# A two-layer hybrid decoder trunk: stick and differential attention in joint steps, stick q and k from stationary weights, the rotation on VectorE

## The chip, the cores and the metric

The kernel runs on one core of one Trainium2 chip. The time is the device time of one execution in microseconds, median of three runs.

## What is computed

x is 256 tokens by 1024, the depth is two layers. All products are float32 in the reference.

```python
f = swiglu(rms_norm(h, ffn1_pre_g[i]), ffn1_w_gu[i], ffn1_w_down[i])
h = h + 0.5 * rms_norm(f, ffn1_post_g[i])
u = rms_norm(h, mix_pre_g[i])
sb_q, sb_k, sb_v, df_q, df_k, df_v, g_sb, g_df = jnp.split(u @ w_in[i], split_at, axis=-1)
o_sb = stick_breaking_attention(sb_q, sb_k, sb_v)      # 8 heads of 64
dq, dk = rope(df_q, positions), rope(df_k, positions)  # 4 heads, 2 x 64
o_df = rms_norm(differential_attention(dq, dk, df_v, lam), ...) * (1.0 - lam_init)
merged = sigmoid(g_sb) * (o_sb @ w_branch_sb[i]) + sigmoid(g_df) * (o_df @ w_branch_diff[i])
h = h + rms_norm(merged @ w_out[i], mix_post_g[i])
```

The second FFN and a gated embedding follow in each layer. Stick attention masks strictly (key before query), differential attention causally (key not after query), with a softmax.

## The kernel before

The engines' programs are written out by hand, with semaphores; the order in the code is the order of each queue. There are 8 PSUM banks of 512 columns. Weights come in units of 2048 columns by 128 rows through three slots. SyncE loads a unit (`raw`), ScalarE writes its rounded high part (`high`, L646, four pieces of 512, scaled by the norm's gain), VectorE the rest (`low`, L1084), and TensorE starts the unit when `split_done` says so (`begin`). A slot is free for ScalarE when TensorE has counted the unit in `units_used`. A product is exact by three passes: high x high, high x low, low x high (`exact`, L1473 to L1475). In the FFN the weights are the stationary side instead (L1591, L1601): a pass of 512 columns takes high weights against both halves of the inputs, a pass of 256 low weights against the high half; the two halves land side by side in a bank and are added later.

The mixer runs units m = 0 to 19 of w_in, two to each block of 512 output columns (j = m // 2), then m = 20 to 27 of the branch and output weights. The blocks are in the order stick q, k, v, diff q, k, v, gates. For q and k, `wide` has the inputs stationary, so the result has tokens as rows. ScalarE copies it to `tmp` (`keep`), scaled by the norm factor of the row. For diff, GpSimd rotates it (`rope`, L577 to L585, in `tmp` and `glu`). TensorE transposes it (`turn_four`, L1692) and ScalarE or VectorE copies the result to `sbq_t`, `sbk_t`, `dfq_t`, `dfk_t`. v is kept by VectorE (L1314).

Small steps stand between the big ones. `middle(i, m)` comes after the first token tile of unit m, `behind(i, m)` after its second. Stick pairs of heads take scores (L1709, L1712), then on ScalarE abs, exp and ln (L792 to L796), on VectorE the cap and the split (L1241 to L1255), then `stick_later` (L1723), the weights (L788), then the values (L1736) and their split `os_hi`, `os_lo`. Two stick steps share banks 0 and 1. A diff head takes a mask matmul (L1698), scores (L1749, L1752), the row maximum on VectorE (L1323), exp on ScalarE (L804), the mix (L1344), the transposes (L1759), their copy `mixed_t` (L813), the values (L1767 to L1770), their squares, GpSimd's scale and VectorE's normed output (L1278).

```python
SB_SCORE = {12 + 6 * n: n for n in range(PAIRS)}
SB_LATER = {15 + 6 * n: n for n in range(PAIRS)}
SB_VALUE = {17 + 6 * n: n for n in range(PAIRS)}
DF_Z0, DF_T0, DF_P0 = 12, 13, 14
```

A stick slot is 2m for `middle` and 2m + 1 for `behind`. The diff heads start every second unit from 12, and the stick pairs every third unit from 6. The mixer's semaphore for ready norm factors is `pre_scale`; GpSimd derives `r_query` from them (`query_scale`, L598).

Of the kernel before, what the change touches and what calls it, by code (L numbers as in the profile page):

```python
# [76 lines left out]
def trunk_kernel(nc, a, out):  # L77
    with ExitStack() as ctx:
# [82 lines left out]
        ident_b = sb("ident_b", [P, P], BF16)  # L161
# [3 lines left out]
        mask_df = sb("mask_df", [P, SEQ], BF16)  # L165
# [15 lines left out]
        slab_c = tmp[:, :, W:D]  # L181

# [42 lines left out]
        kept_dve = sem("kept_dve")  # L225
# [3 lines left out]
        sb_turned = sem("sb_turned")  # L229
# [12 lines left out]
        d_score = sem("d_score")  # L242
        d_max = sem("d_max")
# [71 lines left out]
        OUT_COLS = slice(384, W)  # L315
        both_scores = ps[:, 0:2, 0:384]
        both_outs = ps[:, 0:2, OUT_COLS]
# [68 lines left out]
        def _(sp_):  # L386
# [56 lines left out]
            for i in range(DEPTH):  # L443
# [27 lines left out]
        def _(pool):  # L471
# [33 lines left out]
            for c in (0, P):  # L505

                last = pool.affine_select(out=mask_df[:, c:c + P], in_=mask_df[:, c:c + P],
                                          compare_op=ALU.is_ge, fill=NEG, base=0, pattern=[[-1, P]],
                                          channel_multiplier=1)
            last.then_inc(const_all, 1)  # L510
# [58 lines left out]
            def rope(i, k):  # L569

                for t in range(TT):
                    pool.wait_ge(kept_act, 16 * i + 2 * (2 + k) + t + 1)
                    if k or t:
                        pool.wait_ge(roped, 4 * i + 2 * k + t)
                    x = slab[:, t, :].rearrange("p (g c) -> p g c", c=64)
                    y = rope_b[:, t, :].rearrange("p (g c) -> p g c", c=64)
                    pool.tensor_tensor(slab_c[:, t, :].rearrange("p (g c) -> p g c", c=64), x,  # L577
                                       rope_c[:, t:t + 1, :].to_broadcast([P, 8, 64]), ALU.mult)
                    pool.tensor_tensor(y[:, :, 0:32], x[:, :, 32:64],
                                       rope_s[:, t:t + 1, 0:32].to_broadcast([P, 8, 32]), ALU.mult)  # L580
                    pool.tensor_tensor(y[:, :, 32:64], x[:, :, 0:32],
                                       rope_s[:, t:t + 1, 32:64].to_broadcast([P, 8, 32]), ALU.mult
                                       ).then_inc(rope_parts, 1)
                    pool.wait_ge(rope_parts, 4 * i + 2 * k + t + 1)
                    pool.tensor_tensor(slab[:, t, :], slab_c[:, t, :], rope_b[:, t, :], ALU.add).then_inc(roped, 1)  # L585

            for i in range(DEPTH):
# [11 lines left out]
                pool.wait_ge(rope_ready, 2)  # L599
# [18 lines left out]
        def _(act):  # L618
# [196 lines left out]
            def diff_mid(i, m):  # L815

                if m >= DF_P0 and (m - DF_P0) % 2 == 0 and (m - DF_P0) // 2 < DF_HEADS:
                    hd = (m - DF_P0) // 2
                    act.wait_ge(d_value, DF_HEADS * i + hd + 1)
                    if hd:  # L820
                        act.wait_ge(d_square, DF_HEADS * i + hd)
# [1137 lines left out]
```

## Time and profile before

| what | value |
|---|---|
| median of 3 runs | 1186.8 us (1186.26 to 1187.11) |
| the profiled execution | 1187.24 us |
| its span | 1185.2 us |
| PE busy | 1173.8 us (99%) |
| VectorE (DVE) busy | 848.7 us (72%) |
| ScalarE (ACT) busy | 719.9 us (61%) |
| GpSimd (POOL) busy | 92.9 us (8%) |
| mean granted TensorE clock | 0.999 |

The span goes from the first to the last instruction. Duration of a matmul in a row is from its issue to its modelled end, so neighbours overlap; the distance between starts is what counts. An fp32 matmul of the scores or values stands twice in the trace (four rows for two); a transpose stands once. The first layer's mixer goes from about 205 to 367 us, the second's from about 789 to 952.

### The profile page before, as it was taken

Reading aid. Unit: us, or ns where it says so; the run is one execution under the profiler, and the core shown is the slowest. Engines: PE = TensorE matmul, PEld = TensorE weight load, DVE = VectorE, ACT = ScalarE, POOL = GpSimd, SP = SyncE. Lnnn points to the kernel's source line nnn. Section 1 sums busy time; section 2 is a strip of 40 time slices with the busy share of each in tenths; the row PEclk is TensorE's granted clock in tenths of the full one; section 3 lists DMA queues with packets and bytes.
Section 4 is the critical chain, followed back from the end, with each engine's and each line's share of the span. In section 5 each row is a group of like instructions: output and inputs, shape, how many; then the busy total and the mean of one; then the engine's idle time right before and its main releaser. Section 6 shows DMA issues by size and latency. Waiting matters only on the chain.

```text
span 1185.2 us, 17137 instructions
## 1 busy us (share of the span) xinstructions
PE 1173.8 (99%) x6013; PEld 984.4 (83%) x6013; DVE 848.7 (72%) x1235; ACT 719.9 (61%) x1163; POOL 92.9 (8%) x157
## 2 busy tenths in 40 slices
PE   8999999999999999999999999999999999999997
PEld 7888888888788888888888888888877888888886
DVE  5766777588667866676787776676976776767666
ACT  6655556666665755564685655576656666555555
POOL 4000000042000100000110000010600010000002
PEclk9999999999999999999999999999999999999999
DMA  8656565553345555556546565756343456556550
GB/s 269 232 183 201 171 218 192 198 178 118 132 178 178 178 196 194 191 172 230 178 158 203 175 209 178 249 162 208 114 159 133 169 178 213 175 179 206 183 196 36
DMA packets 138654, 215.36 MB, mean 182 GB/s; under 512 B 6958, under 2 KB 97904, under 8 KB 138608
## 3 DMA queue, kind: packets, MB, share of 16 engines
q1 hardware_dynamic: 135808, 208.43, 52.9%
q10 hardware_dynamic: 2576, 6.29, 1.6%
q8 instruction: 28, 0.46, 0.2%
q14 instruction: 18, 0.15, 0.0%
q0 software_dynamic: 224, 0.04, 0.0%
HBM read 213.68 MB, written 1.05 MB: 181 GB/s over the span
## 4 chain that ended last, share of the span: by engine, by line
PE 96%; ACT 2%; DVE 1%; DMA 1%; issue 0%; POOL 0%; SPq 0%; DVEq 0%; POOLq 0%; ACTq 0%
PE ps L1591 22%; PE ps L1473 19%; PE ps L1475 19%; PE ps L1474 19%; PE ps L1601 12%; PE ps L1520 2%; PE ps L1692 1%; DMA raw<-in_w_ple_proj 1%; PE ps L1723 1%; DVE w_lo L1084 0%; ACT w_hi L646 0%; PE ps L1736 0%; PE ps L1709 0%; ACT prob L804 0%; PE ps L1752 0%
## 5 line engine op out<-in xcount | busy, mean ns | idle before, releaser
L1084 DVE SCALAR_TENSOR_TENSOR w_lo<-raw,g_layer,w_hi 128x512 fp32r<-128x512 f32 (+1 forms) x504 | 369.6, 793 | 131.4 <-ACT w_hi L646 131.4
L646 ACT ACTIVATE w_hi<-raw,g_layer 128x512 fp32r<-128x512 f32 (+1 forms) x524 | 346.9, 732 | 113.5 <-PE ps L1601 97.0
L1591 PE MATMUL ps<-x_both,w_hi 128*128 128x512 f32 x1152 | 287.7, 392 | 0.0
L1473 PE MATMUL ps<-w_hi,x_both 128*128 128x512 f32 x640 | 257.4, 402 | 0.0
L1475 PE MATMUL ps<-w_hi,x_both 128*128 128x512 f32 x640 | 250.2, 391 | 0.0
L1474 PE MATMUL ps<-w_lo,x_both 128*128 128x512 f32 x640 | 249.6, 390 | 0.0
L1591 PEld LDWEIGHTS ps<-x_both,w_hi 128*128 128x128 f32 x1152 | 209.4, 189 | 39.3 <-issue 0.3
L1081 DVE TENSOR_TENSOR w_lo<-raw,w_hi 128x1024 fp32r<-128x1024 f32 x114 | 134.7, 1221 | 55.0 <-ACT w_hi L643 55.0
L643 ACT ACTIVATE w_hi<-raw 128x1024 fp32r<-128x1024 f32 x114 | 114.7, 1052 | 91.7 <-PE ps L1475 91.6
L1601 PEld LDWEIGHTS ps<-x_both,w_lo 128*128 128x128 f32 x1152 | 152.6, 191 | 8.4
L1601 PE MATMUL ps<-x_both,w_lo 128*128 128x256 f32 x1152 | 156.0, 283 | 0.0
L1473 PEld LDWEIGHTS ps<-w_hi,x_both 128*128 128x128 f32 x640 | 120.2, 188 | 27.1 <-issue 3.3
L1475 PEld LDWEIGHTS ps<-w_hi,x_both 128*128 128x128 f32 x640 | 120.1, 188 | 26.1
L1474 PEld LDWEIGHTS ps<-w_lo,x_both 128*128 128x128 f32 x640 | 120.4, 188 | 22.8
L1473 PE MATMUL ps<-w_hi,ht_hi 128*128 128x512 f32 x320 | 124.9, 390 | 0.0
L1475 PE MATMUL ps<-w_hi,ht_lo 128*128 128x512 f32 x320 | 124.6, 389 | 0.0
L1474 PE MATMUL ps<-w_lo,ht_hi 128*128 128x512 f32 x320 | 124.5, 389 | 0.0
L728 ACT ACTIVATE glu<-glu 128x512 f32<-128x512 f32 x36 | 22.8, 633 | 78.5 <-DVE glu L1130 78.5
L1475 PEld LDWEIGHTS ps<-w_hi,ht_lo 128*128 128x128 f32 x320 | 60.1, 188 | 12.5
L1474 PEld LDWEIGHTS ps<-w_lo,ht_hi 128*128 128x128 f32 x320 | 60.1, 188 | 12.4
L1473 PEld LDWEIGHTS ps<-w_hi,ht_hi 128*128 128x128 f32 x320 | 60.1, 188 | 12.3
L536 POOL TENSOR_TENSOR ms_post<-mean_post,eps_half 128x1 f32<-128x1 f32 x8 | 2.4, 305 | 548.6 <-ACT tmp L694 548.6
(217 smaller groups left out, 1008.7 us busy)
## 6 DMA issues: line engine op xcount, KB each, us to landing
raw<-in_ffn_w_gu SPq DMA_DIRECT2D x170, 512.0 KB, 4.6
raw<-in_ffn_w_down SPq DMA_DIRECT2D x88, 512.0 KB, 4.0
raw<-in_w_in SPq DMA_DIRECT2D x80, 512.0 KB, 4.6
raw<-in_w_out SPq DMA_DIRECT2D x16, 512.0 KB, 3.7
raw<-in_w_ple_gate SPq DMA_DIRECT2D x16, 512.0 KB, 4.1
raw<-in_w_branch_sb SPq DMA_DIRECT2D x8, 512.0 KB, 3.7
raw<-in_w_branch_diff SPq DMA_DIRECT2D x8, 512.0 KB, 3.7
raw<-in_ffn_w_gu SPq DMA_DIRECT2D x12, 256.0 KB, 7.6
```

Of the source, the lines that this page charges most:

```text
L643: last = act.activation(w_hi[:, s, part], raw[:, s, part], ACT.Copy)
L646: last = act.activation(w_hi[:, s, part], raw[:, s, part], ACT.Copy, scale=g_layer[:, g:g + 1])
L728: act.activation(glu_g, glu_g, ACT.Silu).then_inc(silu_done, 2)
L1081: last = dve.tensor_tensor(w_lo[:, s, part], raw[:, s, part], whi[:, part], ALU.subtract)
L1084: last = dve.scalar_tensor_tensor(out=w_lo[:, s, part], in0=raw[:, s, part], scalar=g_layer[:, g:g + 1], in1=whi[:, part], op0=ALU.mult, o ...
L1473: pe.matmul(dst, x_h, w_h, start=first, stop=False, **group)
L1474: pe.matmul(dst, x_h, w_l, start=False, stop=False, **group)
L1475: return pe.matmul(dst, x_l, w_h, start=False, stop=last, **group)
L1520: mm = pe.transpose(x_bank(i, q, idx)[:, k * P:(k + 1) * P], src[:, (4 * n + k) * P:(4 * n + k + 1) * P], ident[:, :])
L1591: mm = pe.matmul(dst, w_hi[:, s, cols], x_both[:, :, 4 * half + k, :], start=half == 0 and k == 0, stop=stop and k == 3, skip_group_check= ...
L1601: mm = pe.matmul(bank(FLAT_BANK[j])[:, 0:SEQ], w_lo[:, s, cols], x_hi[:, 4 * half + k, :], start=False, stop=False, skip_group_check=True)
L1692: mm = pe.transpose(dst[:, k * SEQ + t * P:k * SEQ + (t + 1) * P], src[:, t, k * P:(k + 1) * P], ident[:, :])
```

## The change

The blocks of w_in come in another order: diff q, diff k, stick q, stick k, diff v, stick v, gates. The diff products are rotated by VectorE straight from PSUM. Stick q and k are made with the weights stationary, so that they are already transposed; ScalarE copies the second half of the columns (`keep_flat`), VectorE adds the first and multiplies by the norm factors laid out along the free dimension (`add_flat`). These are made by a spread copy on VectorE (`spread_r`), two transposes and a copy (`keep_r`), as in the FFN. The diff mask becomes a minimum on VectorE. v is kept by ScalarE. A stick and a diff step stand at the same place in units 7, 10, 13, 16 (scores) and 9, 12, 15, 18 (transposes and values). The stick values have a bank of their own.

```diff
-SBQ, SBK, SBV, DFQ, DFK, DFV = range(6)
+DFQ, DFK, SBQ, SBK, DFV, SBV = range(6)
+W_IN_BLOCK = (3, 4, 0, 1, 5, 2, 6, 7, 8, 9)
 
 PAIRS = SB_HEADS // 2
-SB_SCORE = {12 + 6 * n: n for n in range(PAIRS)}
-SB_LATER = {15 + 6 * n: n for n in range(PAIRS)}
-SB_VALUE = {17 + 6 * n: n for n in range(PAIRS)}
-DF_Z0, DF_T0, DF_P0 = 12, 13, 14
-BY_ACT = (0, 1, 3, 4, 6, 7, 8, 9)
-QK_ORDER = {SBQ: 0, SBK: 1, DFQ: 2, DFK: 3}
+SB_SCORE = {15 + 6 * n: n for n in range(PAIRS)}
+SB_LATER = {18 + 6 * n: n for n in range(PAIRS)}
+SB_VALUE = {slot_: n for n, slot_ in enumerate((24, 27, 33, 38))}
+DF_SCORE = {7 + 3 * n: n for n in range(DF_HEADS)}
+DF_TURN = {9 + 3 * n: n for n in range(DF_HEADS)}
+BY_ACT = (DFV, SBV, 6, 7, 8, 9)
 
 PIECED = 4
 WARM_UP = (13, 5)
...
-        both_outs = ps[:, 0:2, OUT_COLS]
+
+        SB_FLAT = {SBQ: (0, 4), SBK: (0, 2)}
+        VALUE_BANK = (3, 3, 3, 5)
+
+        def outs(n):
+            return bank(VALUE_BANK[n])[:, 0:SEQ].rearrange("p (t q) -> p t q", t=TT)
+
+        def flat_pair(b):
+            return [ps[:, b:b + 2, n * SEQ:(n + 1) * SEQ] for n in range(2)]
+
+        def nth_r(i, stage):
+
+            return 3 * i + stage + 1
+
 
         def diagonal(b):
...
@@ VectorE
+                                             None, ALU.mult)
+                last.then_inc(d_normed, 1)
+
+            def rope(i, k, t):
+
+                wait_product(dve, win_done, 10 * i + k + 1, i, U_WIN + 2 * k + 1, t)
+                r = (r_query, r_pre)[k][:, t:t + 1]
+                x = bank(WIN_BANK[k][t]).rearrange("p (g c) -> p g c", c=64)
+                y = rope_b[:, t, :].rearrange("p (g c) -> p g c", c=64)
+                dve.scalar_tensor_tensor(out=slab_c[:, t, :].rearrange("p (g c) -> p g c", c=64), in0=x, scalar=r,
+                                         in1=rope_c[:, t:t + 1, :].to_broadcast([P, 8, 64]),
+                                         op0=ALU.mult, op1=ALU.mult)
+                for lo, hi in ((0, 32), (32, 64)):
+                    last = dve.scalar_tensor_tensor(out=y[:, :, lo:hi], in0=x[:, :, 32 - lo:64 - lo], scalar=r,
+                                                    in1=rope_s[:, t:t + 1, lo:hi].to_broadcast([P, 8, 32]),
+                                                    op0=ALU.mult, op1=ALU.mult)
+                last.then_inc(rope_parts, 1)
+                dve.wait_ge(rope_parts, 4 * i + 2 * k + t + 1)
+                dve.tensor_tensor(df_slabs[k][t], slab_c[:, t, :], rope_b[:, t, :], ALU.add).then_inc(roped, 1)
+
+            def add_flat(i, j):
+
+                for x, b in enumerate(SB_FLAT[j]):
+                    n = 4 * i + 2 * (j - SBQ) + x + 1
+                    dst = (sbq_t, sbk_t)[j - SBQ][:, 2 * x:2 * x + 2, :]
+                    dve.wait_ge(flat_kept, n)
+                    dve.scalar_tensor_tensor(out=dst, in0=flat_pair(b)[0], scalar=SB_D ** -0.5 if j == SBQ else 1.0,
+                                             in1=flat_copy, op0=ALU.mult, op1=ALU.add).then_inc(flat_added, 1)
+                    dve.wait_ge(flat_added, n)
+                    dve.wait_ge(r_kept, nth_r(i, 1))
+                    dve.tensor_tensor(dst, dst, r_cols.to_broadcast([P, 2, SEQ]), ALU.mult).then_inc(sb_ready, 1)
+
             def mixer(i):
+                if i == 0:
...
+                dve.wait_ge(pre_scale, 8 * i + 4)
+                dve.wait_ge(query_scale, i + 1)
                 for m in range(23):
 
-                    if m >= DF_P0 and (m - DF_P0) % 2 == 0 and (m - DF_P0) // 2 < DF_HEADS:
-                        hd = (m - DF_P0) // 2
-                        dve.wait_ge(d_scale, DF_HEADS * i + hd + 1)
-                        for t in range(TT):
-                            last = dve.tensor_scalar(o_df[:, t, hd * DF_V:(hd + 1) * DF_V],
-                                                     bank(DF_BANK[1])[:, t * P:(t + 1) * P], r_sub[:, t:t + 1],
-                                                     None, ALU.mult)
-                        last.then_inc(d_normed, 1)
+                    if m in (1, 3):
+                        rope(i, m // 2, 0)
 
...
+                    stick_cap(i, 2 * m)
+
+                    if m in (1, 3):
+                        rope(i, m // 2, 1)
+                    if m == 2:
+                        spread_r(i)
                     if m == 1:
                         dve.wait_ge(lam_loaded, 16 * i + 16)
...
@@ ScalarE
+
+                for x, b in enumerate(SB_FLAT[j]):
+                    n = 4 * i + 2 * (j - SBQ) + x
+                    wait_product(act, win_done, 10 * i + j + 1, i, U_WIN + m, x)
+                    act.wait_ge(flat_added, n)
+                    act.activation(flat_copy, flat_pair(b)[1], ACT.Copy, scale=SB_D ** -0.5 if j == SBQ else 1.0
+                                   ).then_inc(flat_kept, 1)
 
             def keep(i, m):
 
...
@@ TensorE
-                    pe.wait_ge(os_split, PAIRS * i + n)
+                    pe.wait_ge(s_weight, PAIRS * i + n)
                 for e, rows in enumerate(HEAD_ROWS):
...
-                    turn_four(pair(QK_PAIR), slab).then_inc(qk_turned, 1)
-                if m == 9:
+                    pe.wait_ge(r_kept, nth_r(i, 1))
                     pe.wait_ge(roped, 4 * i + 2)
-                    pe.wait_ge(sb_turned, 2 * i + 2)
-                    turn_four(pair(QK_PAIR), slab).then_inc(qk_turned, 1)
-                if m == 11:
+                    turn_four(pair(QK_PAIR), df_slabs[0]).then_inc(qk_turned, 1)
+                if m == 6:
                     pe.wait_ge(roped, 4 * i + 4)
                     pe.wait_ge(df_turned, 2 * i + 1)
-                    turn_four(pair(QK_PAIR), slab).then_inc(qk_turned, 1)
+                    turn_four(pair(QK_PAIR), df_slabs[1]).then_inc(qk_turned, 1)
                 stick(i, 2 * m + 1)
-                if 0 <= m - DF_Z0 < 2 * DF_HEADS and (m - DF_Z0) % 2 == 0:
-                    diff_scores(i, (m - DF_Z0) // 2)
-                if 0 <= m - DF_T0 < 2 * DF_HEADS and (m - DF_T0) % 2 == 0:
-                    diff_turn(i, (m - DF_T0) // 2)
+                if m in DF_SCORE:
...
+            def flat_win(i, m, j, half, x):
+
+                s, b = slot(U_WIN + m), SB_FLAT[j][x]
+                if half == 0:
+                    if x:
+                        pe.wait_ge(rope_parts, 4 * i + 2 * (j - SBQ) + 2)
+                    elif j == SBK:
+                        pe.wait_ge(flat_added, 4 * i + 1)
+
+                def long(stop):
...
```

`flat_win` issues for each half unit and each pair of 128 columns eight passes of 512 and eight of 256 columns, as the FFN's L1591 and L1601 do. Its second pair waits for the rotation that read the same banks, and the first pair of stick k for VectorE's first add of stick q:

```python
if half == 0:
    if x:
        pe.wait_ge(rope_parts, 4 * i + 2 * (j - SBQ) + 2)
    elif j == SBK:
        pe.wait_ge(flat_added, 4 * i + 1)
```

TensorE at the end of unit 2, first layer. Before:

```order
L1473 MATMUL ps<-w_hi,x_both 128x512
L1474 MATMUL ps<-w_lo,x_both 128x512
L1475 MATMUL ps<-w_hi,x_both 128x512
L1692 MATMUL ps<-ident,tmp 128x128 [waits kept_act]
L1692 MATMUL ps<-ident,tmp 128x128 x7
L1473 MATMUL ps<-w_hi,x_both 128x512 [waits split_done]
L1474 MATMUL ps<-w_lo,x_both 128x512
```

and now:

```order
L1504 MATMUL ps<-w_hi,x_both 128x512
L1505 MATMUL ps<-w_lo,x_both 128x512
L1506 MATMUL ps<-w_hi,x_both 128x512
L1578 MATMUL ps<-ident,mixed_t 128x128 [waits r_wide]
L1578 MATMUL ps<-ident,mixed_t 128x128
L1504 MATMUL ps<-w_hi,x_both 128x512 [waits split_done]
L1505 MATMUL ps<-w_lo,x_both 128x512
```

The eight transposes of `tmp` (scaled stick q) are gone from here; two of the spread norm factors stand in their place and wait for VectorE's copy.

VectorE from the last split of the mixer's inputs on, first layer. Before (L1109 is that split):

```order
L1109 TENSOR_TENSOR x_both<-ps,x_both 128x4x128
L1084 SCALAR_TENSOR_TENSOR w_lo<-raw,g_layer,w_hi 128x512 x4
L1298 TENSOR_TENSOR lam_pr<-lam_layer 128x128
L1301 TENSOR_REDUCE lam_s<-lam_pr 128x2
L1084 SCALAR_TENSOR_TENSOR w_lo<-raw,g_layer,w_hi 128x512 x12
L1304 TENSOR_TENSOR neg_lam<-lam_e 128x1
L1307 TENSOR_TENSOR neg_lam<-neg_lam,neg_init 128x1
L1084 SCALAR_TENSOR_TENSOR w_lo<-raw,g_layer,w_hi 128x512 x4
```

and now (L1102 is that split, L1278 to L1287 a rotation, L1113 the spread copy):

```order
L1102 TENSOR_TENSOR x_both<-ps,x_both 128x4x128
L1278 SCALAR_TENSOR_TENSOR tmp<-ps,r_query,rope_c 128x512
L1282 SCALAR_TENSOR_TENSOR glu<-ps,r_query,rope_s 128x8x32 x2
L1287 TENSOR_TENSOR tmp<-tmp,glu 128x512
L1077 SCALAR_TENSOR_TENSOR w_lo<-raw,g_layer,w_hi 128x512 x4
L1278 SCALAR_TENSOR_TENSOR tmp<-ps,r_query,rope_c 128x512
L1282 SCALAR_TENSOR_TENSOR glu<-ps,r_query,rope_s 128x8x32 x2
L1287 TENSOR_TENSOR tmp<-tmp,glu 128x512
L1335 TENSOR_TENSOR lam_pr<-lam_layer 128x128
L1338 TENSOR_REDUCE lam_s<-lam_pr 128x2
L1077 SCALAR_TENSOR_TENSOR w_lo<-raw,g_layer,w_hi 128x512 x4
L1113 COPY mixed_t<-r_pre 128x256
```

Two rotations have moved ahead of the low parts of units 3 and 4, and the copy for which TensorE waits stands behind both.

TensorE at the end of unit 7, where the first scores now are, behind the flat product of stick k. Before, the first scores stood behind unit 6:

```order
L1473 MATMUL ps<-w_hi,x_both 128x512
L1474 MATMUL ps<-w_lo,x_both 128x512
L1475 MATMUL ps<-w_hi,x_both 128x512
L1709 MATMUL ps<-sbq_t,sbk_t 128x256 [waits sb_turned]
L1709 MATMUL ps<-sbq_t,sbk_t 128x256
L1712 MATMUL ps<-sbq_t,sbk_t 128x128 x2
L1473 MATMUL ps<-w_hi,x_both 128x512 [waits kept_act]
```

and now:

```order
L1866 MATMUL ps<-x_both,w_hi 128x512 x8
L1875 MATMUL ps<-x_both,w_lo 128x256 x8
L1866 MATMUL ps<-x_both,w_hi 128x512 x8
L1738 MATMUL ps<-sbq_t,sbk_t 128x256 [waits sb_ready]
L1738 MATMUL ps<-sbq_t,sbk_t 128x256
L1741 MATMUL ps<-sbq_t,sbk_t 128x128 x2
L1778 MATMUL ps<-dfk_t,dfq_t 128x128 [waits df_turned]
L1778 MATMUL ps<-dfk_t,dfq_t 128x128
L1781 MATMUL ps<-dfk_t,dfq_t 128x256 x2
```

Stick scores now wait for VectorE's scaled k, and the diff scores follow at once, without mask matmuls.

## Rows read from the trace of the kernel before

**Rows 1.** Page, section 1: busy us (share), instructions of each engine.

```profile
PE 1173.8 (99%) x6013; PEld 984.4 (83%) x6013; DVE 848.7 (72%) x1235; ACT 719.9 (61%) x1163; POOL 92.9 (8%) x157
```

**Rows 2.** The page, section 4: the chain that ended last, shares by engine.

```profile
PE 96%; ACT 2%; DVE 1%; DMA 1%; issue 0%; POOL 0%; SPq 0%; DVEq 0%; POOLq 0%; ACTq 0%
```

**Rows 3.** Waits, PE: engine, line <- releaser: us in total, times, longest.

```profile
PE ps L1767 <- ACT mixed_t L813: 0.4, 2, 0.2
```

**Rows 4.** First mixer: us, busy PE PEld DVE ACT POOL, clock, DMA, GB/s.

```profile
208.33:344.14 135.81, 135.60 (x709) 109.19 (x707) 97.67 (x150) 91.48 (x176) 25.17 (x28) 1.00 0.47 159
```

**Rows 5.** Timeline, PE, units 2 to 4: start, us from first to last, instructions.

```profile
218.43 0.39 PE L1475 MATMUL ps<-w_hi,x_both 128*128 128x512 f32 x1
218.66 1.03 PE L1692 MATMUL ps<-ident,tmp 128*128 128x128 f32 x8
219.45 0.48 PE L1473 MATMUL ps<-w_hi,x_both 128*128 128x512 f32 x1
...
230.47 1.03 PE L1692 MATMUL ps<-ident,tmp 128*128 128x128 f32 x8
```

**Rows 6.** Timeline, PE, units 12 to 14; [idle before <-releaser].

```profile
284.39 0.39 PE L1698 MATMUL ps<-mask_df,ident_b 128*128 128x256 bf16 x2
284.71 0.38 PE L1749 MATMUL ps<-dfk_t,dfq_t 64*128 64x128 f32 x2
...
307.79 0.48 PE L1473 MATMUL ps<-w_hi,x_both 128*128 128x512 f32 x1
311.01 0.49 PE L1767 MATMUL ps<-v_df,mixed_t 128*128 128x128 f32 x2 [0.21 <-ACT mixed_t L813]
311.33 0.39 PE L1768 MATMUL ps<-v_df,mixed_t 128*128 128x128 f32 x2
311.56 0.39 PE L1770 MATMUL ps<-v_df,mixed_t 128*128 128x128 f32 x2
```

**Rows 7.** Chain in order of time, second FFN of layer 0: start, us, what.

```profile
431.28 1.81 PE ps L1591 x8
...
442.43 0.23 PE ps L1473
```

**Rows 8.** Timeline, POOL, the first mixer.

```profile
211.22 0.20 POOL L598 TENSOR_TENSOR r_query<-r_pre,q_factor 128x2 f32<-128x2 f32 x1
```

**Rows 9.** Timeline, DVE, the first mixer.

```profile
212.93 2.74 DVE L1084 SCALAR_TENSOR_TENSOR w_lo<-raw,g_layer,w_hi 128x512 fp32r<-128x512 f32 x4 [2.94 <-ACT w_hi L646]
...
215.91 0.29 DVE L1301 TENSOR_REDUCE lam_s<-lam_pr 128x2 f32<-128x128 f32 x1
...
246.44 4.78 DVE L1084 SCALAR_TENSOR_TENSOR w_lo<-raw,g_layer,w_hi 128x512 fp32r<-128x512 f32 x4
```

**Rows 10.** Groups by form, DVE, windows 20:60, 375:410, 208:352.

```profile
L1147 DVE SCALAR_TENSOR_TENSOR glu<-ps,r_pre,glu 128x256 f32<-128x256 f32 x2 | 1.0, 479 | 0.0
...
L1120 DVE COPY mixed_t<-r_pre 128x256 f32<-128x256 f32 x1 | 0.3, 284 | 0.0
...
L1185 DVE TENSOR_TENSOR tmp<-ps,post_g 128x512 f32<-128x512 f32 x4 | 2.7, 686 | 2.5 <-ACT tmp L694 2.5
...
L1241 DVE SCALAR_TENSOR_TENSOR soft<-ps,soft 128x768 f32<-128x768 f32 x4 | 3.8, 956 | 4.1 <-ACT soft L796 4.1
```

**Rows 11.** Timeline, ACT, units 1 to 3.

```profile
211.56 2.56 ACT L646 ACTIVATE w_hi<-raw,g_layer 128x512 fp32r<-128x512 f32 x4
...
219.73 1.03 ACT L876 ACTIVATE sbq_t<-ps 128x1024 f32<-128x1024 f32 x1 [2.01 <-PE ps L1692]
...
225.22 0.69 ACT L842 ACTIVATE tmp<-ps,r_pre 128x512 f32<-128x512 f32 x1 [1.35 <-PE ps L1475]
```

**Rows 12.** Windows, the end of the program (columns as in rows 4).

```profile
1177.90:1180.00 2.10, 0.01 (x1) 0.00 (x0) 1.50 (x4) 1.91 (x5) 0.00 (x0) 1.00 0.46 170
...
1182.00:1183.00 1.00, 0.00 (x0) 0.00 (x0) 0.69 (x2) 0.00 (x0) 0.00 (x0) 1.00 0.11 43
1183.00:1184.00 1.00, 0.00 (x0) 0.00 (x0) 0.00 (x0) 0.00 (x0) 0.00 (x0) 0.50 1.02 381
```

More of the change, by code:

```diff
@@ L181, in trunk_kernel @@
         slab_c = tmp[:, :, W:D]
+        df_slabs = [[x[:, t, 0:W] for t in range(TT)] for x in (tmp, gates[:, 0, :, :])]
+        flat_copy = w_att[:, :, 0:SEQ]
         minus = mixed_t[:, 0:P]
@@ new lines, in diff_keep, with diff_square @@
+            def diff_keep(i, hd):
+                act.wait_ge(d_turned, DF_HEADS * i + hd + 1)
+                act.activation(mixed_t[:, :], bank(DF_BANK[0])[:, 0:384], ACT.Copy).then_inc(d_kept, 1)
+            def diff_square(i, hd):
+                act.wait_ge(d_value, DF_HEADS * i + hd + 1)
+                if hd:
+                    act.wait_ge(d_square, DF_HEADS * i + hd)
+                for t in range(TT):
+                    last = act.activation(squares[:, t * P:(t + 1) * P], bank(DF_BANK[1])[:, t * P:(t + 1) * P],
+                                          ACT.Square, scale=DF_V ** -0.5, accum_out=mean_sub[:, t:t + 1])
+                last.then_inc(d_square, 1)
@@ L1745, in diff_scores @@
                     pe.wait_ge(d_normed, DF_HEADS * i + hd)
-                for c in range(2):
-                    masked(DF_BANK[c], mask_df)
                 for c, rows in enumerate(HEAD_ROWS):
-                    pe.matmul(bank(DF_BANK[c])[:, 0:P], dfq_t[rows, hd, 0:P], dfk_t[rows, hd, 0:P], start=False,
+                    pe.matmul(bank(DF_BANK[c])[:, 0:P], dfq_t[rows, hd, 0:P], dfk_t[rows, hd, 0:P], start=True,
                               stop=False, skip_group_check=True)
@@ new lines, in flat_win, with short @@
+            def flat_win(i, m, j, half, x):
[6 more added lines that the diff above has]
+                def long(stop):
+                    for n in range(2):
+                        dst = bank(b + n).rearrange("p (a n) -> p a n", a=2)
+                        for k in range(4):
+                            cols = slice(k * W + (2 * x + n) * P, k * W + (2 * x + n + 1) * P)
+                            mm = pe.matmul(dst, w_hi[:, s, cols], x_both[:, :, 4 * half + k, :],
+                                           start=half == 0 and k == 0, stop=stop and k == 3, skip_group_check=True)
+                    return mm
+                def short():
+                    for n in range(2):
+                        for k in range(4):
+                            cols = slice(k * W + (2 * x + n) * P, k * W + (2 * x + n + 1) * P)
+                            mm = pe.matmul(bank(b + n)[:, 0:SEQ], w_lo[:, s, cols], x_hi[:, 4 * half + k, :],
+                                           start=False, stop=False, skip_group_check=True)
+                    return mm
+                if half == 0:
+                    long(False)
+                    return short()
+                short()
+                mm = long(True)
+                if x == 0:
+                    mm.then_inc(win_done, 1)
+                return mm
@@ L1838, in mixer @@
                     for t in range(TT):
-                        if half == 0 and j >= 2:
-                            kept(i, j - 2, t)
+                        if j in SB_FLAT:
+                            mm = flat_win(i, m, j, half, t)
+                            if t == 0:
+                                middle(i, m)
+                            continue
+                        if half == 0:
+                            bank_free(i, j, t)
                         mm = wide(slot(U_WIN + m), bank(WIN_BANK[j % 2][t]), x_hi, x_lo, 4 * half, t,
```

237 lines of the change are left out of this document (104 added, 133 removed).

## The prediction

> **What bounds the kernel now.** I read the page's shares first. TensorE's matmuls are busy 1173.8 of 1185.2 us, VectorE 72%, ScalarE 61% [rows 1]. The chain that ended last runs 96% on PE [rows 2], and the longest waits of PE after the start are two of 0.2 us [rows 3]. So a microsecond of TensorE work that leaves the program is a microsecond gained, and work on the other three engines costs nothing until TensorE stands still for it. In the first layer's mixer the same: 135.60 of 135.81 us busy, with VectorE at 97.67 and ScalarE at 91.48 [rows 4]. These two have room on average, so the question is where their order makes TensorE wait.
>
> A matmul of 512 columns takes 0.227 us from start to start [rows 5], a unit of w_in (24 of them) 5.45 us. Every burst of small matmuls also slows what follows: 48 matmuls took 11.02 us between two sets of transposes [rows 5], 0.14 more than 48 x 0.227 = 10.88.
>
> **What TensorE loses, per layer.** (a) The stick q and k transposes: eight in 0.79 us [rows 5], twice: -1.58. (b) The mask matmuls, 0.32 us for a head [rows 6], four times: -1.28. (c) Joint steps: the order rows give 24 bursts between the end of unit 2 and unit 21 before and 17 after; 7 x 0.14 = -0.98. (d) The pause of 0.21 us before the second head's values, and the same head's slow stretch (12 matmuls take 3.22 from 307.79 to 311.01 where 12 x 0.227 + 0.14 is 2.86) [rows 6]. Scores now have a unit and a half to their transposes instead of one, so I take both as gone: -0.21 - 0.35 = -0.56. (e) Added: the two transposes of the row factor, 0.79/8 each [rows 5]: +0.2. (f) Stick q and k from stationary weights: 32 matmuls of 512 columns and 32 of 256 in place of 48 of 512, the same number of columns. In the FFN such a pair of units takes from 431.28 to 442.43, 11.15 us [rows 7], so 5.57 a unit against 5.45; four units: +0.5. Sum: -1.58 - 1.28 - 0.98 - 0.56 + 0.2 + 0.5 = -3.70 us.
>
> The Trainium skill, "TensorE: Matmul & The Clock Gate", section "Back-to-back issue gap", gives N/2.4 + 2.5 ns between starts, so 216 ns for 512 columns and 109 for 256. By it (f) would be +0.04 instead of +0.5 and the time of both layers about 0.9 lower. The rows have 0.227 us for 512 columns and 5.57 for the flat unit, and I keep them.
>
> **What the others gain or lose.** GpSimd loses the rotation. Four low parts of VectorE took 4.78 us at 246.44, where four otherwise take 2.74 [rows 9]; the first rotation was running on GpSimd then. No wait of TensorE hung on these, so silence on GpSimd is worth nothing on the path. ScalarE loses eight copies of 0.69 and two of 1.03 us and gets four v copies and four half copies of 0.69 and two diff copies of 1.03 [rows 11]: even. VectorE gets three things. One rotation of a token tile is one three-operand operation of 512, two of 256, a wait and a sum of 512. Near rows: four three-operand 512s in 2.74, so 0.67 each; 0.48 for 256 from PSUM, 0.69 for a two-operand 512 from PSUM, both measured to the end and about 0.09 less from start to start [rows 9, 10]. That makes 0.67 + 0.39 + 0.48 + 0.04 (the wait) + 0.60 = 2.2 us. Bounds, as the strided form with a factor table is nowhere in the trace: 1.8 (two halves at 0.28, the cost of a 256 copy) and 3.3 (0.96, the 768 form from PSUM, and halves at 0.75). It also gets the add and scale of stick q and k, and the two minima for the mask, both off the path except as below. The minima (0.48 each at most, the 256 form) lie in the one and a half units between scores and transposes.
>
> **Where TensorE now stands still, per layer.** (g) *The row factor.* TensorE's next step after unit 2 is its transposes, which wait for VectorE's spread copy. In the order rows two rotations, two units' low parts and the lambda steps stand ahead of that copy. VectorE can start when r_query is there: 211.22 + 0.20 = 211.4 [rows 8], with unit 0's product long ready. Then 2.2 (rotation), 2.66 (low), 2.2, 0.6 (lambda: from the low parts' end at 215.6 to 215.91 + 0.29), 2.66, 0.28 (copy) [rows 9, 10]: 10.6, so 222.1. ScalarE's high parts for these units start at 211.56 and take 2.56 each [rows 11], so they are no later. Unit 2 ends at 218.66 [rows 5], where the old transposes began. TensorE waits 3.5 us. Behind it are all later units. By the bounds of the rotation the wait is 2.7 to 5.7.
> (h) *The first half of stick k.* It goes to PSUM banks 0 and 1, which VectorE's first add of q must have read. From the end of unit 4: transposes 0.79, unit 5 5.57, so TensorE is there at 6.4. ScalarE copies diff q (starts 0.28 behind the transposes, as the old copy at 219.73 did, and takes 1.03) until 2.1, makes the high part of a unit until 4.6 (2.56), then the half copy (0.68). VectorE needs the second half of the high part for its last two low pieces, until 6.0, then the add, 0.7: 6.7. Wait 0.3.
> (i) *The first scores.* The same chain behind unit 6, and the scale on top (0.68): 7.4 against 6.4. Wait 1.0.
> (j) *The values of the first head.* They need v of the second token tile, whose product is the last thing of the same unit. ScalarE starts 0.26 behind the product [rows 11], takes 0.69, 0.05 for the signal; the first two pairs cover 0.46 (0.23 from 311.33 to 311.56, twice) [rows 6]. Wait 0.55. Before, VectorE had kept it a unit earlier.
> Later units: ScalarE's work stays at some 91 us in some 135. VectorE's goes from 97.67 to at most 116 us: + 4 x 2.2, + 4 x (0.67 + 0.69), + 8 x 0.48, the copies and GpSimd's disturbance that it loses not counted [rows 4, 9, 10]. Both are now spread over evenly spaced joint steps, so I count no wait there.
> Waits: 3.5 + 0.3 + 1.0 + 0.55 = 5.35 us. (g) could end the others if it gave ScalarE and VectorE a lead, but the chains of (h), (i) and (j) start from TensorE's own last product, so they go late with it.
>
> **Sum.** 5.35 - 3.70 = +1.65 us a layer, +3.3 for two (the order of the second layer's mixer is the same). The profiled execution took 1187.24; with 3.3 it is 1190.5. The median of the runs is 0.44 below that execution, so **1190.1 us**.
>
> **Rivals.** *A, not slower: only the row factor is waited for.* (h), (i) and (j) are small differences of long chains; a gap of 1 us vanishes if the high part or a signal is that much earlier. For it: before, no such chain ever reached TensorE [rows 3]. Against: the order leaves ScalarE no choice. It decides where the add ends within 6.4 us of unit 6. Then 3.5 - 3.70 = -0.2 a layer: 1186.4. With the rotation at its lower bound (2.7) it is 1184.8, and if the missing bursts save half as much again (1.0 us in all), 1183.8. Chance 0.33.
> *B, the clock falls in the gap.* At the end of the program TensorE's last matmul is over at 1177.9 and the granted clock is still 1.00 (2.4 GHz) until 1183, then 0.50 (1.2 GHz) [rows 12]: it fell after about 5 us of idleness. The new gap is 3.5 to 5.7 us. If it falls, the unit behind the gap (5.45 us) runs at half speed in whole or in part, 2.7 us a layer at half of it: 1195.5. The Trainium skill, "TensorE: Matmul & The Clock Gate", section "Part 1: The HAM clock gate", says that an idle array goes back to the half rate; by this rule B holds and the forecast doesn't, and only the row's 5 us speaks for no fall. Chance 0.12.
> *C, VectorE is the bound through units 3 to 9.* Rotations of 3.3 us make the wait at (g) 5.7 and push (h) and (i) by nothing more, since the rotations of k are over by then: +2.2 a layer, 1194.5. Chance 0.10.
> *D, an unpriced gain*, such as fewer slow starts behind the bursts: 1183. Chance 0.05.
> That the change does not do what it says is excluded by the order rows; the forecast keeps 0.40.
>
> **How the numbers follow.** A measurement can tell 0.2% (2.4 us) from no change, so slower begins above 1189.2. Of the forecast, whose own range is 1188 to 1192.5, 0.35 lie there and 0.05 below; B and C add 0.22: slower 0.57. Of A 0.20 lies within 0.2%: same 0.25. A's lower part, 0.13, and D: faster 0.18. The range, 1183.8 to 1195.8, goes from A's lower end to B.
>
> **What would show it.** In the new profile: a pause of PE of 3 to 4 us ahead of the transposes of mixed_t in each mixer, released by VectorE's copy; under 2 us makes (g) wrong. Rotations of 2.2 us. PE pauses of some tenths ahead of unit 6 and about 1 us ahead of the first scores, released by VectorE's add and scale, and about half a microsecond within the first head's values, released by ScalarE's v copy. No matmul on the mask. A granted clock of 1.00 through the gap. No PE gap at the first transposes would overthrow the forecast altogether, and the time would be below 1184.

## The result, and the profile after

The changed kernel takes 1190.92 us in the median of 7 runs (1189.29 to 1191.23), the kernel before 1186.79 us beside it (7 runs, 1186.26 to 1187.22). The ratio is 1.0032, with a 95% interval of 1.0022 to 1.0042: slower by 0.3%, 0.8 us above the forecast of 1190.1 and inside its range. The profiled execution took 1190.49 us, with a span of 1188.8. In three of 20 runs of the kernel before, taken beside the experiments, and in three of the ten with the mask on VectorE, the mean granted clock is 0.001 to 0.002 lower and the time about 2 us longer; none of them was profiled, and the medians are little moved by them.

Page of the changed kernel, section 1 and the chain of section 4, which answer to [rows 1] and [rows 2]:

```profile
PE 1168.9 (98%) x6033; PEld 985.5 (83%) x6033; DVE 850.1 (72%) x1289; ACT 720.1 (61%) x1165; POOL 51.1 (4%) x122
PE 94%; DVE 3%; ACT 1%; issue 1%; DMA 1%; POOL 0%; SPq 0%; DVEq 0%; POOLq 0%; ACTq 0%
```

TensorE is busy 4.9 us less than before and the program is longer all the same: it now stands still for others. VectorE has 3% of the chain, where it had 1%. Waits of PE in the mixers, in us: total, times, longest. All four are new; the kernel before had one wait in its mixers, 0.4 in all [rows 3].

```profile
PE ps L1578 <- DVE mixed_t L1113: 6.5, 2, 3.3
PE ps L1738 <- DVE sbk_t L1299: 1.7, 2, 0.8
...
PE ps L1800 <- ACT v_df L833: 0.7, 2, 0.3
...
PE ps L1866 <- DVE sbq_t L1295: 0.4, 2, 0.2
```

These are the forecast's (g), (i), (j) and (h). A wait counts from the modelled end of the last matmul, some 0.16 us after the next one could have started; from start to start the stops are longer by that.

The two mixers, cut at the same instructions as [rows 4] and with its columns:

```profile
207.93:347.11 139.18, 134.48 (x718) 110.81 (x717) 99.83 (x178) 92.20 (x178) 4.65 (x12) 0.98 0.46 157
795.83:932.21 136.38, 131.79 (x718) 108.84 (x717) 99.89 (x178) 92.21 (x178) 4.67 (x12) 1.00 0.47 160
```

Before, the first took 135.81 [rows 4] and the second 135.76 by the same cut. So the first layer (layer 0) loses 3.37 us and the second (layer 1) 0.62, with the same instructions in both. The column of the granted clock, the share of the full 2.4 GHz that TensorE was given, tells them apart: 0.98 and 1.00.

The stop itself, the idle stretch of TensorE ahead of the row factor's transposes, timeline of PE in layer 0 and then in layer 1 (start, us, engine, line, operation, count, idle before and who ended it):

```profile
218.03 0.39 PE L1506 MATMUL ps<-w_hi,x_both 128*128 128x512 f32 x1
221.72 0.69 PE L1578 MATMUL ps<-ident,mixed_t 128*128 128x128 f32 x2 [3.30 <-DVE mixed_t L1113]
...
223.06 0.63 PE L1506 MATMUL ps<-w_hi,x_both 128*128 128x512 f32 x1
223.49 0.63 PE L1504 MATMUL ps<-w_hi,x_both 128*128 128x512 f32 x1
...
809.51 0.44 PE L1578 MATMUL ps<-ident,mixed_t 128*128 128x128 f32 x2 [3.20 <-DVE mixed_t L1113]
...
810.25 0.40 PE L1506 MATMUL ps<-w_hi,x_both 128*128 128x512 f32 x1
810.49 0.39 PE L1504 MATMUL ps<-w_hi,x_both 128*128 128x512 f32 x1
```

From 218.03 + 0.23 to 221.72 the engine is idle for 3.46 us; in layer 1 its last matmul starts at 805.93, and the stop is 3.35. Behind the stop matmuls start every 0.43 us in layer 0, every 0.23 in layer 1. What VectorE had queued ahead of the copy, its timeline in the same stretch:

```profile
211.22 0.75 DVE L1278 SCALAR_TENSOR_TENSOR tmp<-ps,r_query,rope_c 128x512 f32<-128x512 f32 x1 [1.63 <-POOL r_query L588]
211.88 0.87 DVE L1282 SCALAR_TENSOR_TENSOR glu<-ps,r_query,rope_s 128x256 f32<-128x256 f32 x2
212.79 0.69 DVE L1287 TENSOR_TENSOR tmp<-tmp,glu 128x512 f32<-128x512 f32 x1
213.40 2.73 DVE L1077 SCALAR_TENSOR_TENSOR w_lo<-raw,g_layer,w_hi 128x512 fp32r<-128x512 f32 x4
216.05 0.74 DVE L1278 SCALAR_TENSOR_TENSOR tmp<-ps,r_query,rope_c 128x512 f32<-128x512 f32 x1
...
218.22 0.28 DVE L1335 TENSOR_TENSOR lam_pr<-lam_layer 128x128 f32<-128x128 f32 x1
...
218.74 2.73 DVE L1077 SCALAR_TENSOR_TENSOR w_lo<-raw,g_layer,w_hi 128x512 fp32r<-128x512 f32 x4
221.38 0.28 DVE L1113 COPY mixed_t<-r_pre 128x256 f32<-128x256 f32 x1
```

A rotation takes 213.40 - 211.22 = 2.18 us. VectorE never idles from 211.22 on, and the copy is the last of its queue. The granted clock across the stop (columns as above):

```profile
219.00:220.00 1.00, 0.00 (x0) 0.00 (x0) 1.00 (x2) 0.00 (x0) 0.00 (x0) 1.00 1.05 408
220.00:221.00 1.00, 0.00 (x0) 0.00 (x0) 1.00 (x3) 0.00 (x0) 0.00 (x0) 0.81 0.47 180
221.00:222.00 1.00, 0.28 (x2) 0.28 (x3) 0.67 (x2) 0.00 (x0) 0.00 (x0) 0.50 0.00 0
...
227.00:228.00 1.00, 1.00 (x5) 0.82 (x4) 0.43 (x1) 0.00 (x0) 0.00 (x0) 0.78 0.00 0
```

A share of 0.81 means 0.38 us at half rate, so the clock fell at about 220.6, some 2.4 us into the stop, and came back at about 227.4. The price: units 3 and 4 took 13.64 us in layer 0, 11.11 in layer 1.

```profile
222.06:235.70 13.64, 13.64 (x59) 11.34 (x57) 8.06 (x14) 5.49 (x10) 0.00 (x0) 0.80 0.37 121
809.71:820.82 11.11, 11.11 (x58) 9.50 (x58) 8.01 (x14) 5.49 (x10) 0.00 (x0) 1.00 0.46 147
```

That is 2.53 us. The two transposes ahead of them took 0.34 instead of 0.20, so the price is 2.67, once in the program. The mean granted clock of the seven runs is 0.995 or 0.996, and that of every run with the stop filled (below) 0.998 or 0.999. A fall of 6.8 us lowers the mean by 0.003, so each of the seven fits one such fall, and none fits two.

### The profile page after: what moved, and what is told of

It is laid out like the page before. It is cut to its first block, busy times and chain, and to the rows that moved or that the text cites. A ratio compares the mean times of both kernels' runs of the same rounds, so it can differ in the third digit from the quotient of the medians.

```text
span 1188.8 us, 17199 instructions
## 1 busy us (share of the span) xinstructions
PE 1168.9 (98%) x6033; PEld 985.5 (83%) x6033; DVE 850.1 (72%) x1289; ACT 720.1 (61%) x1165; POOL 51.1 (4%) x122
## 4 chain that ended last, share of the span: by engine, by line
PE 94%; DVE 3%; ACT 1%; issue 1%; DMA 1%; POOL 0%; SPq 0%; DVEq 0%; POOLq 0%; ACTq 0%
PE ps L1625 22%; PE ps L1504 18%; PE ps L1506 18%; PE ps L1505 18%; PE ps L1635 12%; DVE w_lo L1077 2%; PE ps L1551 2%; PE ps L1866 1%; PE ps L1875 1%; PE ps L1752 1%; DMA raw<-in_w_ple_proj 1%; PE ps L1767 1%; ACT w_hi L633 0%; PE ps L1726 0%; PE ps L1738 0%
## 5 line engine op out<-in xcount | busy, mean ns | idle before, releaser
L1077 DVE SCALAR_TENSOR_TENSOR w_lo<-raw,g_layer,w_hi 128x512 fp32r<-128x512 f32 (+1 forms) x504 | 355.9, 766 | 140.3 <-ACT w_hi L633 140.3
L1504 PE MATMUL ps<-w_hi,x_both 128*128 128x512 f32 x576 | 232.0, 403 | 0.0
L1506 PE MATMUL ps<-w_hi,x_both 128*128 128x512 f32 x576 | 226.1, 393 | 0.0
L1505 PE MATMUL ps<-w_lo,x_both 128*128 128x512 f32 x576 | 225.6, 392 | 0.0
L630 ACT ACTIVATE w_hi<-raw 128x1024 fp32r<-128x1024 f32 x114 | 114.7, 1052 | 92.9 <-PE ps L1506 92.8
L1504 PEld LDWEIGHTS ps<-w_hi,x_both 128*128 128x128 f32 x576 | 109.0, 189 | 24.0 <-issue 3.0
L1506 PEld LDWEIGHTS ps<-w_hi,x_both 128*128 128x128 f32 x576 | 108.7, 189 | 23.5
L1505 PEld LDWEIGHTS ps<-w_lo,x_both 128*128 128x128 f32 x576 | 109.0, 189 | 20.9
L1125 DVE TENSOR_TENSOR glu<-glu,prob 128x512 f32<-128x512 f32 x36 | 24.9, 691 | 27.6 <-ACT glu L715 27.6
```

The lines of the kernel that those rows point to most:

```text
L630: last = act.activation(w_hi[:, s, part], raw[:, s, part], ACT.Copy)
L1077: last = dve.scalar_tensor_tensor(out=w_lo[:, s, part], in0=raw[:, s, part], scalar=g_layer[:, g:g + 1], in1=whi[:, part], op0=ALU.mult, o ...
L1125: dve.tensor_tensor(glu_g, glu_g, wide_r, ALU.mult).then_inc(silu_scaled, 1)
L1504: pe.matmul(dst, x_h, w_h, start=first, stop=False, **group)
L1505: pe.matmul(dst, x_h, w_l, start=False, stop=False, **group)
L1506: return pe.matmul(dst, x_l, w_h, start=False, stop=last, **group)
```

## The experiments

The runs with the copy first, with the stop filled, with the mask on VectorE in the kernel before, and with the other waits taken away were timed on one chip beside the kernel before at 1187.38 us (20 runs). The other three, with no mask, with the mask back on TensorE and with the copy behind the second rotation, were timed on another beside it at 1187.23 (15 runs). The changed kernel had stood beside it at 1186.79. Medians of different sets are therefore good to some 0.6 us against each other, and where less than that matters the mixers are compared, cut in the traces as above.

**The copy ahead of the rotations.** From the changed kernel, VectorE's order only:

```diff
                 for m in range(23):
+                    if m == 1:
+                        spread_r(i)
                     if m in (1, 3):
                         rope(i, m // 2, 0)
...
-                    if m == 2:
-                        spread_r(i)
```

> The changed kernel with VectorE's spread copy of the norm factors moved from behind the low part of unit 4 to ahead of the first rotation. Theory (the row-factor wait is a wait of its own, and the clock's fall is its consequence): no PE wait ahead of the two transposes, which cost 3.5 us in each layer, and no granted clock under 1.00 in the mixers, which cost 2.5 us in the layer where it fell; everything else on VectorE 0.3 us later. 1190.9 - 7.0 - 2.5 = 1181.4 us, down to 1179 if the clock usually fell twice. Rival (VectorE is simply behind through units 1 to 7, so the wait moves on): PE waits for the low part of unit 3 or 4 or longer for stick q and k, and the time stays at 1184 us or above.

Measured: 1181.32 us (1180.77 to 1181.62), ratio to the kernel before 0.9947 [0.9933, 0.9961]. TensorE no longer waits for the row factor, the other three waits are unchanged, and the clock is 1.00 in both mixers. Against the changed kernel 9.6 us are gone by the medians, and 10.2 if each is taken against the kernel before beside it. The mixers decide: they take 132.97 and 133.01 us, 6.21 and 3.37 less than in the changed kernel, 9.58 together, where the stops of 3.46 and 3.35 and the fall's 2.67 make 9.48. One copy of 0.28 us, put behind 10 us of other work, turned the change from a gain into a loss.

**The stop filled.** TensorE gets 22 matmuls of 256 columns on data it has, with a result that nobody reads, ahead of the row factor's transposes:

```diff
                 if m == 2:
+                    for _ in range(22):
+                        pe.matmul(bank(7)[:, 0:SEQ], x_hi[:, 0, 0:P], x_hi[:, 1, :], start=True, stop=True,
+                                  skip_group_check=True)
```

> The changed kernel with 22 extra matmuls of 256 columns (results unused) ahead of the two row-factor transposes, about 2.6 us of the 3.5 us gap. It separates the clock from the wait. If the clock's fall is caused by the idleness in the gap: granted clock 1.00 in both mixers, the wait shrinks to under 1 us but the transposes start when they did, and the time falls by 2.5 us for each fall, 1188.4 or 1186 us. If the clock had fallen for another reason: 0.50 behind the gap again and about 1190.9 us.

Measured: 1188.2 us (11 runs, 1187.74 to 1188.55), ratio 1.0005 [0.9996, 1.0014]. Timeline of PE, and the window behind the stop, of this kernel:

```profile
218.34 2.79 PE L1821 MATMUL ps<-x_both 128*128 128x256 f32 x22
221.82 0.44 PE L1578 MATMUL ps<-ident,mixed_t 128*128 128x128 f32 x2 [0.68 <-DVE mixed_t L1113]
```

```profile
222.00:224.00 2.00, 2.00 (x11) 1.66 (x11) 0.00 (x0) 1.70 (x4) 0.00 (x0) 1.00 0.62 121
```

The transposes start at 221.82 as before (221.72), since VectorE's queue is the same, but the clock stays at 1.00. By the medians 2.7 us come back, and 3.3 if each is taken against the kernel before beside it. In the traces the first mixer takes 136.55 instead of 139.18, 2.63 less, and the second 136.42 instead of 136.38. So the fall is caused by TensorE's idleness in the stop and is worth some 2.7 us by itself, apart from the stop.

**The mask on VectorE, alone, in the kernel before.** This tests term (b) by itself: the two mask matmuls of a head leave TensorE, the two minima come to VectorE ahead of its maximum, and nothing else changes.

```diff
-                for c in range(2):
-                    masked(DF_BANK[c], mask_df)
...
+                        for c in range(2):
+                            last = dve.tensor_tensor(diagonal(DF_BANK[c]), diagonal(DF_BANK[c]),
+                                                     cap_df[:, :, :].to_broadcast([P, 2, P]), ALU.min)
+                        last.then_inc(d_capped, 1)
+                        dve.wait_ge(d_capped, DF_HEADS * i + hd + 1)
```

> The kernel before with the diff mask alone moved from TensorE (two bf16 matmuls a head) to two minima on VectorE. Theory (a microsecond off TensorE is a microsecond gained): 8 heads x 0.32 = 2.6 us less, 1184.2 us. Rival (the minima, 0.8 us, lengthen the chain from scores to transposes, which has only one unit here): a wait ahead of the transposes eats up to 0.8 us a head, and the time stays between 1185.5 and 1187 us. By the trace of before the slack is 0.7 to 2 us, so I expect 1184.2 to 1184.6.

Measured: 1190.81 us (10 runs, 1189.79 to 1192.72), ratio 1.0031 [1.0022, 1.0041]. The expectation missed by 6.6 us and by its sign. Waits of PE:

```profile
PE ps L1775 <- ACT mixed_t L818: 3.3, 2, 1.6
...
PE ps L1757 <- DVE glu L1283: 1.1, 2, 0.5
PE ps L1767 <- DVE mixed L1354: 0.6, 2, 0.3
```

And the chain that ended last, in order of time, behind the first scores (start, us, what):

```profile
284.91 0.46 PE ps L1760 x4
...
285.39 0.78 DVE ps L1328 x2
...
286.19 1.03 DVE neg_max L1333 x2
...
287.25 1.73 ACT prob L809 x8
...
289.11 2.55 ACT w_hi L651 x4
291.66 0.85 ACT gates L850 x2
...
293.50 0.38 ACT mixed_t L818
```

From the scores over minima (0.78), maximum, exponential and ScalarE's next high part to the kept product, which the values wait for, and on over the squares, GpSimd's scale and VectorE's normed output (`glu`, L1283) to the next head's scores. In the kernel before a head has one unit from scores to transposes, and the wait of 0.2 us there [rows 3] already said that this chain had no room. The minima lengthen it. This is a second limit beside TensorE's own work that the shares of the page do not show; the next run tests it.

**No mask at all, in the kernel before.** The same edit without the minima; it leaves the causal mask of the differential scores out.

> The kernel before without any mask of the differential attention, neither the two mask matmuls nor minima; it leaves the causal mask of those scores out. If the kernel before with the mask on VectorE lost because its minima lengthen the chain from the scores to the next unit's scores, then without them the 8 x 0.32 = 2.6 us of mask matmuls are gained in full: 1184.2 to 1184.8. Rival: the chain is already as long as TensorE's work between two units, so that taking matmuls away uncovers it: 1186 to 1187, and waits of TensorE for the mixed product appear as large as what was taken away. If 1190, the minima had nothing to do with it.

Measured: 1185.58 us (11 runs, 1184.7 to 1185.81), ratio 0.9984 [0.9975, 0.9993]: 1.65 us faster.

```profile
PE ps L1770 <- ACT mixed_t L818: 1.1, 2, 0.6
```

The first diff scores of the kernel before, behind their mask that starts at 284.39 [rows 6], up to the next big matmul, and then the same of this run:

```profile
285.57 0.50 PE L1473 MATMUL ps<-w_hi,x_both 128*128 128x512 f32 x1
```

```profile
284.84 0.49 PE L1752 MATMUL ps<-dfk_t,dfq_t 64*128 64x128 f32 x4
...
285.69 0.50 PE L1478 MATMUL ps<-w_hi,x_both 128*128 128x512 f32 x1
```

That is 1.18 us with the mask and 0.85 without: in the kernel before it costs TensorE 0.33 a head, as forecast. The time lies between the two expectations. The wait for the kept product grows from 0.4 to 1.1, so of the 2.6 us taken from TensorE 0.7 come straight back: -1.9 by these two, -1.65 measured. The run with the minima is 5.2 us above this one by the medians and by the mixers; its waits add up to 3.9 us more, and four more stops of 0.16 make 4.5. The remaining 0.7 is open.

**The mask back on TensorE, among the joint steps.** The fastest version (below) with two bf16 mask matmuls a head as before and no minima:

```diff
-                        for c in range(2):
-                            last = dve.tensor_tensor(diagonal(DF_BANK[c]), diagonal(DF_BANK[c]),
-                                                     cap_df[:, :, :].to_broadcast([P, 2, P]), ALU.min)
...
+                for c in range(2):
+                    masked(DF_BANK[c], mask_df)
```

> The fastest version so far (copy ahead of the rotation, the flat rows kept ahead of the high and low parts) with the differential mask back on TensorE as two bf16 matmuls a head, the minima gone. If moving the mask is a gain among the joint steps, where VectorE has a unit and a half between them, this costs 8 x 0.32 = 2.6 us: 1178.2 + 2.6 = 1180.8. Rival: the minima cost in the chain of waits what the matmuls cost on TensorE, as in the kernel before: no change, 1178.2, or faster.

Measured: 1182.8 us (1182.43 to 1183.25), ratio 0.9962 [0.9949, 0.9976]: 4.6 us slower than without the mask matmuls, not 2.6. The mixers are 2.23 and 2.21 us longer, 4.4 together. A joint burst, in which a stick and a diff step follow each other, of the fastest version, and then the same burst of this one, timelines of PE:

```profile
269.54 0.39 PE L1747 MATMUL ps<-sbq_t,sbk_t 64*128 64x128 f32 x4
269.76 0.39 PE L1784 MATMUL ps<-dfk_t,dfq_t 64*128 64x128 f32 x4
269.98 0.60 PE L1787 MATMUL ps<-dfk_t,dfq_t 64*128 64x256 f32 x4
```

```profile
270.05 0.39 PE L1757 MATMUL ps<-sbq_t,sbk_t 64*128 64x128 f32 x4
270.37 0.39 PE L1743 MATMUL ps<-mask_df,ident_b 128*128 128x256 bf16 x2
270.69 0.49 PE L1796 MATMUL ps<-dfk_t,dfq_t 64*128 64x128 f32 x4
271.02 0.60 PE L1799 MATMUL ps<-dfk_t,dfq_t 64*128 64x256 f32 x4
```

From the start of the stick scores' last four to the start of the diff scores' last four it is 0.44 us without the mask (269.54 to 269.98) and 0.97 with it (270.05 to 271.02): 0.53 a head. The mask's own pair is 0.32 from start to start; the matmuls of 64 rows on either side each start 0.1 later than they do beside their like. Eight heads make 4.2 of these 4.4 to 4.6.

**The copy behind the second rotation.** From the changed kernel, one line:

```diff
-                    if m == 2:
+                    if m == 1:
                         spread_r(i)
```

> The row factor's spread copy moves only to behind the second rotation of unit 4, ahead of the 2.73 us low part. If TensorE's gap is what is queued ahead of the copy on VectorE, it shrinks by that low part and no more: 3.46 - 2.7 = about 0.8 us per layer, the clock stays at 1.00, and the time is that of the run with the copy ahead of the rotation (1181.3) plus the rotation twice over, 2 x 0.8: 1182.9. Rival: if the clock falls in any gap at this place, or if the factor waits for something other than the queue, the wait stays at 3 us or the clock at half: 1188 or more.

Measured: 1181.95 us (1181.4 to 1182.38), ratio 0.9953 [0.994, 0.9967]. It is 0.63 above the run with the copy first, where 1.6 was expected. Timelines of PE and of VectorE:

```profile
218.42 0.39 PE L1506 MATMUL ps<-w_hi,x_both 128*128 128x512 f32 x1
218.95 0.44 PE L1578 MATMUL ps<-ident,mixed_t 128*128 128x128 f32 x2
```

```profile
218.61 0.28 DVE L1113 COPY mixed_t<-r_pre 128x256 f32<-128x256 f32 x1
218.81 0.28 DVE L1335 TENSOR_TENSOR lam_pr<-lam_layer 128x128 f32<-128x128 f32 x1
```

The stop is 218.95 - 218.42 - 0.23 = 0.30 us, not 0.8. I had counted only the low part as passed, but the lambda steps stand behind the copy too: 218.74 - 218.22 = 0.52 in the changed kernel. 3.46 - 2.64 - 0.52 = 0.30, and two of these are the 0.6 measured (the mixers are 0.40 and 0.23 longer). The stop is what is queued ahead of the copy, to a tenth of a microsecond.

**The other waits.** From the run with the copy first: ScalarE and VectorE take the first half of each flat unit of stick q and k as soon as it is there, ahead of the next unit's high and low parts, instead of both halves behind them.

```diff
+                    if m in (5, 7):
+                        add_flat(i, m // 2, (0,))
...
                     if m in (5, 7):
-                        add_flat(i, m // 2)
+                        add_flat(i, m // 2, (1,))
```

> As e1_spread_first, and in units 5 and 7 ScalarE copies the first half of stick q or k before the high part of the unit, and VectorE adds and scales it before the low part. Theory (the waits ahead of unit 6, 0.22 us, and ahead of the first scores, 0.84 us, come from the high part standing first in the chain): both go, 2.1 us for two layers less than e1, about 1179.3 us. Rival (ScalarE now waits for the product and its later high parts come late): the high and low parts of unit 7 or 9 reach TensorE late, and the time is that of e1 or above.

Measured: 1178.23 us (1177.97 to 1178.74), ratio 0.9921 [0.9908, 0.9935]. The waits (h) and (i) are gone, and of the four new ones 0.7 us for v is left. It is 3.1 us faster than the copy alone; the two waits were 2.1 as listed, and 2.7 with 0.16 for each of their four stops, and the mixers are 1.38 and 1.40 shorter, 2.8 together. This is the fastest version, ahead of both kernels.

## Why the prediction was right

The time, the sign and the likeliest case were right. The waits were the strong part. Beside them stand two errors of opposite sign, savings too small by 1.8 us and a fall of the clock of 2.7 us left out, which mostly hid each other.

**What bounds the kernel: right, with a gap.** TensorE's own work sets the time, and what leaves it is gained. In the kernel before there is a second limit close behind, the ring through ScalarE in the middle of the mixer. The changed kernel shows no wait for it; its joint steps give a head a unit and a half.

**(g) to (j), the waits: right.** Forecast 3.5, 0.3, 1.0, 0.55, together 5.35 us a layer. Measured from start to start 3.46, 0.38, 1.0, 0.49: 5.33 in layer 0, and 5.22 in layer 1, where (g) is 3.35. The rotation was put at 2.2 us from its nearest rows and takes 2.18. A slip in (g) did no harm: its terms add up to 222.0 and a wait of 3.3, and not to 222.1 and 3.5. Two experiments then took (g), (h) and (i) away by order alone; (j) was left. Rival A, which let (h), (i) and (j) vanish, is refuted by their rows; C, a rotation of 3.3 us, by 2.18.

**(a) to (f), TensorE's savings: direction right, size too small.** Forecast 3.70 a layer. The undisturbed second mixer says 5.22 - 0.62 = 4.60. What was mis-sized is (b) and (c) together, since the forecast priced each as if the other did not matter. By itself (b) is right: the mask costs 0.33 a head in the kernel before, and 0.32 was forecast [rows 6]. In a joint burst it costs 0.53, by the two timelines above. So joined scores save 0.21 a head more once the mask is gone from between them than the 0.14 of (c), 0.84 a layer of the missing 0.90. The last 0.06 is open. Rival D named fewer slow starts as a gain without a price; it is 1.8 us in both layers, where D's 1183 wanted 7. The price behind a burst in (c) holds: 36 matmuls take 257.19 to 265.49, 8.30, that is 0.13 over 36 x 0.227, and the first mixers have 24 and 17 bursts, as counted from the order rows. (e) holds too: the factor's transposes take 0.20 (809.51 to 809.71). And (f), the flat unit, forecast at 5.57, in the fastest version:

```profile
224.03 1.98 PE L1872 MATMUL ps<-x_both,w_hi 128*128 128x512 f32 x8
...
229.59 0.60 PE L1732 MATMUL ps<-ident,tmp 128*128 128x128 f32 x4
```

5.56 us. The row of the FFN was the better guide. (The +0.04 that the prediction sets beside +0.5 is the sum for two units; for the four of (f) it is +0.08, and the time 0.8 lower instead of 0.9.)

**"A granted clock of 1.00 through the gap": wrong in layer 0.** Rival B had the mechanism and the price, 2.7 us a layer, but in both layers (1195.5); it was given 0.12, because the one row on idleness showed 5 us before the clock fell [rows 12]. It fell 2.4 us into one stop of 3.46 and not in the other. The Trainium skill, "TensorE: Matmul & The Clock Gate", section "Part 1: The HAM clock gate", says that an idle array goes back to the half rate; by this rule the trace agrees in layer 0 and shows no fall in layer 1. The mistake was to read one duration as a limit.

**The sum.** Waits and savings by themselves give 2 x 0.62 = 1.2 us more than before, a time of about 1188.0 and within the 0.2% that the forecast counts as no change; the fall adds 2.7. The run with the stop filled (1188.2, ratio 1.0005) is this kernel without the fall. That the forecast of 1190.1 lay so near is in that part luck. The two mixers together are 3.99 us longer, the profiled executions differ by 3.25. Of the 0.7 between, 0.40 is there before the first mixer starts (207.93 against 208.33), because the first weights' DMA took 6.93 us instead of 7.32; 0.35 lies outside the spans (1.69 us against 2.04). Between and behind the mixers the two kernels agree to 0.02.

**Silence on GpSimd:** its work fell from 92.9 to 51.1 us [rows 1], and nothing shows on the path, as said.

## What to carry to other kernels

When work moves to an engine that has room on average, look at what small thing the bound engine waits for next on that engine, and put that ahead of the moved work: here one line of order was worth 9.6 us, and the order of two half copies another 3.1. Price a removed instruction by the start-to-start times of its neighbours with and without it, in the place where they will stand: the same mask cost 0.33 us a head alone and 0.53 in a joint burst. A wait of 0.2 us in the profile can mark a chain without room. Here eight pairs of minima of 0.78 us, on an engine at 72%, made the kernel 5.2 us longer, twice what the mask matmuls had cost TensorE.

## What the runs showed of the hardware

- The granted clock fell to half some 2.4 us into an idle stop of TensorE and stayed there for 6.8 us, until 227.4, with TensorE busy without a break from 221.72 on. In layer 1 a stop of 3.35 us, with the same instructions before it, brought no fall, and at the program's end about 5 us of idleness passed before one [rows 12]. So the length of a stop alone does not tell whether the clock falls; what else decides was not tried.
- At the half rate matmuls of 512 columns started every 0.427 us (eleven steps from 222.64 to 227.33), against 0.227 at full rate: 1.9 times. The Trainium skill, "TensorE: Matmul & The Clock Gate", section "Wait — 56ns, not 53.3ns?", gives 426.7 ns at the low rate, and the trace agrees; at the high rate it gives 215.7 ns, where the rows have 227.
- In these bursts a group of small matmuls of 64 rows is over 0.1 us sooner when the one before is also of 64 rows: 0.22 us from start to start for four of 128 columns, 0.32 where a bf16 group of 128 rows or a burst's first entry stands between.
